# Prompt softmax in a hybrid attention decoder: the reciprocals' spread goes through memory, and the outputs are multiplied in SBUF

## The reference

```python
p, m, den = _softmax_stats(s, sink)        # p = exp(s - max), den = its sum (+ the sink's share)
o = jnp.einsum('nbcgqs,nbscd->nbqcgd', p.astype(vc.dtype), vc, preferred_element_type=jnp.float32)
o = o / jnp.transpose(den, (0, 1, 4, 2, 3))[..., None]
```

## Time and profile before

| what | us |
|---|---|
| median of three runs (lowest, highest) | 2282.36 (2281.73, 2285.25) |
| the profiled execution's own time | 2281.3 |
| its span in the profile | 2279.5 |
| TensorE busy | 2218.8 |
| VectorE busy | 961.8 |
| ScalarE busy | 658.9 |
| GpSimd busy | 137.5 |

### The profile page before, as it was taken

How to read it: one execution, slowest core, us unless ns; L and a number is a source line. 1 busy time by engine, 2 the same in 40 slices (tenths; PEclk the granted TensorE clock), 3 DMA queues, 4 the chain that set the end, 5 groups by cost and what they waited for, 6 DMA issues and landing times.

```text
span 2279.5 us, 33504 instructions
## 1 busy us (share of the span) xinstructions
PE 2218.8 (97%) x13723; PEld 1996.8 (88%) x13723; DVE 961.8 (42%) x1694; ACT 658.9 (29%) x1293; POOL 137.5 (6%) x216
## 2 busy tenths in 40 slices
PE   6999999898999999999999999989999999999998
PEld 6999877686789989899898998889989899898996
DVE  4120386575643424334243345663424334243346
ACT  4111496543432203122031223451303113031121
POOL 1000130000120000000000003330000000000001
PEclk9999999999999999999999999999999999999999
DMA  5230400398321202012020123230202102021023
GB/s 167 80 86 29 158 2 2 114 404 291 102 93 46 65 10 74 27 46 64 9 74 25 49 92 110 89 102 28 66 9 74 46 28 65 9 74 45 29 90 119
DMA packets 127934, 176.15 MB, mean 77 GB/s; under 512 B 14365, under 2 KB 96469, under 8 KB 127708
## 3 DMA queue, kind: packets, MB, share of 16 engines
q1 hardware_dynamic: 121644, 170.05, 22.7%
q10 hardware_dynamic: 6192, 4.72, 0.7%
HBM read 156.40 MB, written 18.58 MB: 77 GB/s over the span
## 4 chain that ended last, share of the span: by engine, by line
PE 76%; DMA 2%; DVE 1%; SPq 1%; issue 0%; ACT 0%; POOL 0%; DVEq 0%; POOLq 0%; ACTq 0%
PE ps L1731 33%; PE ps L1711 33%; PE ps L2606 4%; DMA sa_va<-cache_a_v 1%; PE ps L2555 1%; PE ps L2574 1%; PE ps L1390 1%; PE ps L1720 1%; PE ps L1447 1%; PE ps L1410 0%; DVE m_xT_lo L2361 0%; PE ps L2626 0%; DMA sa_kb<-cache_b_k 0%; SPq L654 0%; PE ps L1430 0%
## 5 line engine op out<-in xcount | busy, mean ns | idle before, releaser
L1675 DVE TENSOR_TENSOR t_y<-t_y,ps 128x512 f32<-128x512 f32 x288 | 197.7, 687 | 626.4 <-PE ps L1731 626.2
L1731 PE MATMUL ps<-t_w_hi,t_h_hi 128*128 128x512 f32 x1152 | 449.7, 390 | 2.9 <-DVE t_h_hi L1652 2.2
L1731 PE MATMUL ps<-t_w_lo,t_h_hi 128*128 128x512 f32 x1152 | 448.4, 389 | 0.0
L1731 PE MATMUL ps<-t_w_hi,t_h_lo 128*128 128x512 f32 x1024 | 398.4, 389 | 0.0
L1711 PE MATMUL ps<-m_xT_lo,t_w_hi 128*128 128x384 f32 x1488 | 327.9, 328 | 0.0
L1711 PE MATMUL ps<-m_xT_hi,t_w_lo 128*128 128x384 f32 x1488 | 327.9, 328 | 0.0
L1711 PE MATMUL ps<-m_xT_hi,t_w_hi 128*128 128x384 f32 x1488 | 327.8, 328 | 0.0
L1606 ACT ACTIVATE t_relu<-ps 128x384 f32<-128x384 f32 (+1 forms) x192 | 87.9, 458 | 809.4 <-PE ps L1731 776.7
L1636 DVE TENSOR_TENSOR t_w_lo<-t_raw,t_w_hi 128x1024 fp32r<-128x1024 f32 x128 | 155.4, 1224 | 276.5 <-ACT t_w_hi L1594 276.1
L1731 PEld LDWEIGHTS ps<-t_w_hi,t_h_hi 128*128 128x128 f32 x1152 | 216.2, 188 | 50.9 <-DVE t_h_hi L1652 3.1
L1711 PEld LDWEIGHTS ps<-m_xT_hi,t_w_hi 128*128 128x128 f32 x1488 | 254.7, 188 | 1.1
(11 more groups left out here) (224 smaller groups left out, 2476.0 us busy)
## 6 DMA issues: line engine op xcount, KB each, us to landing
t_raw<-mlp_w SPq DMA_DIRECT2D x128, 512.0 KB, 4.0
sa_kb<-cache_b_k SPq DMA_DIRECT2D x40, 512.0 KB, 8.9
sa_vb_even<-cache_b_v SPq DMA_DIRECT2D x20, 512.0 KB, 11.3
sa_vb_odd<-cache_b_v SPq DMA_DIRECT2D x20, 512.0 KB, 10.9
in_raw<-attn_w_in SPq DMA_DIRECT2D x6, 1024.0 KB, 5.6
t_rows<-scratch_x SPq DMA_DIRECT2D x12, 512.0 KB, 5.2
qT<-x_prompt SPq DMA_DIRECT2D x8, 512.0 KB, 3.6
t_rows<-x_prompt SPq DMA_DIRECT2D x8, 512.0 KB, 3.4
```

The source lines that it names most:

```text
L1675: self.nc.vector.tensor_tensor(part, part, self.core.ps[:, 6 + n % 2, :], ALU.add).then_inc(self.part_added, 1)
L1731: mm = self.nc.tensor.matmul(self.core.ps[:, 6 + half, :], a[:, k, t * P:t * P + P], w[:, k, half * 512:(half + 1) * 512], start=(k == 0 a ...
```

## The change

The spread groups leave the list of groups, and with them the four transposes, ScalarE's copy and the repeating copy. In a round, VectorE makes the reciprocals of 8 sums for 128 queries; SyncE waits for them, stores them turned (8 rows of 128, element by element) in a scratch tensor in memory, waits for the store's landing, and issues two loads which bring four rows each, repeated on 64 partitions, into `spread`. VectorE takes the outputs from PSUM by a plain copy into `qT`, and multiplies them there in place with `spread` in a new function, `normalise`, at the step u + 12 for a round that closes at unit u (or at the last step, 133). SyncE's new loop stands behind `load_early`. The number of other groups stays 112, their order stays, and their numbers, and so their places in the batches and PSUM banks, shift.

```diff
@@ -681,7 +681,7 @@
     leading_parts: object
 
 
-def prompt_attention(core, inp, qT, qT_offset, kaT, kbT, v, prompt_bias, sinks, load_sample, q_b, q_a):
+def prompt_attention(core, inp, qT, qT_offset, kaT, kbT, v, prompt_bias, sinks, load_sample, q_b, q_a, rden_rows):
 
 
 
@@ -710,8 +710,7 @@
     pT = core.at("pa_pT", base + Attend.PT, [P, 4, 4 * P])
     least = core.at("pa_least", base + Attend.LEAST, [P, PT, HEADS])
     den = core.at("pa_den", base + Attend.LEAST + 512, [P, PT, HEADS])
-    rden = core.at("pa_rden", base + Attend.LEAST + 1024, [P, NH * HD])
-    rden_one = core.at("pa_rden_one", base + Attend.SINK + 64, [P, 2 * PT, NH])
+    rden = core.at("pa_rden", base + Attend.SINK + 64, [P, 2 * PT, NH])
     spread = core.at("pa_spread", base + Attend.SPREAD, [P, 2, 4 * P])
     sink_in = core.sem("pa_sink_in")
     tables_in = [core.sem(f"pa_tables_in{x}") for x in range(3)]
@@ -722,8 +721,9 @@
     biased = core.sem("pa_biased")
     exped = core.sem("pa_exped")
     rden_made = core.sem("pa_rden_made")
-    rden_ready = core.sem("pa_rden_ready")
-    spread_ready = core.sem("pa_spread_ready")
+    rden_stored = core.sem("pa_rden_stored")
+    spread_in = [core.sem(f"pa_spread_in{x}") for x in range(2)]
+    normalised = core.sem("pa_normalised")
     turned = core.sem("pa_turned")
     copied = [core.sem("pa_copied_act"), core.sem("pa_copied_dve")]
     multiplied = core.sem("pa_multiplied")
@@ -761,18 +761,6 @@
     groups = []
     for u in range(0, U, 2):
         groups += [(u, g, min(2, n_tiles(u) - g)) for g in range(0, n_tiles(u), 2)]
-        if u + 1 in closing:
-            groups.append((u, 0, 0))
-
-    def is_spread(n):
-
-        return groups[n][2] == 0
-
-    spread_index = [n for n in range(len(groups)) if is_spread(n)]
-
-    def before(n):
-
-        return sum(not is_spread(m) for m in range(n))
 
     of_pair = {}
     for n, (u, _, _) in enumerate(groups):
@@ -828,20 +816,22 @@
         return u if wide(u) else u - 2
 
 
-    copier = [int(n % 2 == 1 and k > 0) for n, (u, _, k) in enumerate(groups)]
+    copier = [n % 2 for n in range(len(groups))]
     rounds = {u: x for x, u in enumerate(closing)}
 
-    def group_of(n):
-
-        return rounds[groups[n][0] + 1]
+    normalised_at = {}
+    for u in closing:
+        normalised_at.setdefault(min(u + 12, STEPS), []).append(u)
+
+    def outputs(u):
+
+        i, j, _ = parts_of(u)
+        group = j // 4
+        return qT[:, 4 * group:4 * group + 4, i * P:(i + 1) * P]
 
     def wait_for_copy(n):
 
-        if is_spread(n):
-            nc.tensor.wait_ge(spread_ready, group_of(n) + 1)
-        else:
-            mine = [copier[m] for m in range(n + 1) if not is_spread(m)]
-            nc.tensor.wait_ge(copied[copier[n]], mine.count(copier[n]))
+        nc.tensor.wait_ge(copied[copier[n]], copier[:n + 1].count(copier[n]))
 
 
     pieces = []
@@ -893,6 +883,16 @@
             sp.dma_start(bias_low[:, :, c], table_b[:, 0:5, c]).then_inc(tables_in[x], 16)
             sp.dma_start(bias_high[:, :, c], table_b[:, 5:NH, c]).then_inc(tables_in[x], 16)
         load_sample(sp)
+        for x in range(len(closing)):
+            sp.wait_ge(rden_made, x + 1)
+            sp.dma_start(rden_rows[x].rearrange("d q -> q d"), rden[:, x, :],
+                         allow_slow_non_contiguous=True).then_inc(rden_stored, 16)
+            sp.wait_ge(rden_stored, 16 * (x + 1))
+            if x >= 2:
+                sp.wait_ge(normalised, x - 1)
+            for half in range(2):
+                sp.dma_start(spread[half * HD:(half + 1) * HD, x % 2, :].rearrange("p (j c) -> p j c", j=4),
+                             rden_rows[x, half::2].partition_broadcast(HD)).then_inc(spread_in[x % 2], 16)
 
     def gpsimd(pool):
         for n in range(len(pieces)):
@@ -922,16 +922,9 @@
         def copy(n):
             u, _, k = groups[n]
             act.wait_ge(turned, n + 1)
-            if is_spread(n):
-                x = group_of(n)
-                if x >= 2:
-                    act.wait_ge(o_taken, x - 1)
-                nc.scalar.activation(spread[:, x % 2, :], core.ps[:, 4 + n % 2, :], ACT.Copy).then_inc(spread_ready, 1)
-                return
-            m = before(n)
-            if m >= 4:
-                act.wait_ge(multiplied, m - 3)
-            nc.scalar.activation(pT[:, m % 4, 0:2 * k * P], core.ps[:, 4 + n % 2, 0:2 * k * P],
+            if n >= 4:
+                act.wait_ge(multiplied, n - 3)
+            nc.scalar.activation(pT[:, n % 4, 0:2 * k * P], core.ps[:, 4 + n % 2, 0:2 * k * P],
                                  ACT.Copy).then_inc(copied[0], 1)
 
         act.wait_ge(inp.q_taken, inp.columns)
@@ -955,14 +948,18 @@
         def take_outputs(u):
 
             i, j, _ = parts_of(u)
-            group = j // 4
-            dve.wait_ge(multiplied, before(turned_after(u)))
+            dve.wait_ge(multiplied, turned_after(u))
+            dve.wait_ge(lo_done, lo_pieces(piece_no[i, j - 1] + 1))
+            nc.vector.tensor_copy(outputs(u), core.ps[:, 6 + j // 4, :].rearrange("p (j c) -> p j c", j=4)).then_inc(
+                o_taken, 1)
+
+        def normalise(u):
+
             x = rounds[u]
-            dve.wait_ge(spread_ready, x + 1)
-            dve.wait_ge(lo_done, lo_pieces(piece_no[i, j - 1] + 1))
-            nc.vector.tensor_tensor(qT[:, 4 * group:4 * group + 4, i * P:(i + 1) * P],
-                                    core.ps[:, 6 + group, :].rearrange("p (j c) -> p j c", j=4),
-                                    spread[:, x % 2, :].rearrange("p (j c) -> p j c", j=4), ALU.mult).then_inc(o_taken, 1)
+            dve.wait_ge(o_taken, x + 1)
+            dve.wait_ge(spread_in[x % 2], 32 * (x // 2 + 1))
+            nc.vector.tensor_tensor(outputs(u), outputs(u), spread[:, x % 2, :].rearrange("p (j c) -> p j c", j=4),
+                                    ALU.mult).then_inc(normalised, 1)
 
         dve.wait_ge(sink_in, 16)
         nc.vector.tensor_scalar(neg_sink[:], sink_b[:], -1.0, None, ALU.mult).then_inc(sink_ready, 1)
@@ -990,27 +987,21 @@
             for n in (n for batch in batches_at(step) for n in batch):
                 if copier[n] == 1:
                     dve.wait_ge(turned, n + 1)
-                    m = before(n)
-                    if m >= 4:
-                        dve.wait_ge(multiplied, m - 3)
+                    if n >= 4:
+                        dve.wait_ge(multiplied, n - 3)
                     k = groups[n][2]
-                    nc.vector.tensor_copy(pT[:, m % 4, 0:2 * k * P],
+                    nc.vector.tensor_copy(pT[:, n % 4, 0:2 * k * P],
                                           core.ps[:, 4 + n % 2, 0:2 * k * P]).then_inc(copied[1], 1)
             if step - 2 in closing:
                 x = rounds[step - 2]
                 i, j, _ = parts_of(step - 2)
                 d = 2 * j + 2 - NH
                 dve.wait_ge(exped, step - 1)
-                one = rden_one[:, x, :]
-                nc.vector.reciprocal(one, den[:, i, d:d + NH]).then_inc(rden_made, 1)
-                if x >= 1:
-                    dve.wait_ge(turned, spread_index[x - 1] + 1)
-                dve.wait_ge(rden_made, x + 1)
-                nc.vector.tensor_copy(rden[:].rearrange("p (h d) -> p h d", h=NH),
-                                      one.rearrange("p (h o) -> p h o", o=1).to_broadcast([P, NH, HD])
-                                      ).then_inc(rden_ready, 1)
+                nc.vector.reciprocal(rden[:, x, :], den[:, i, d:d + NH]).then_inc(rden_made, 1)
             for u in taken_at.get(step, ()):
                 take_outputs(u)
+            for u in normalised_at.get(step, ()):
+                normalise(u)
 
     def tensor(pe):
         def scores(u):
@@ -1043,13 +1034,6 @@
             u, g, k = groups[n]
             if n >= 2:
                 wait_for_copy(n - 2)
-            if is_spread(n):
-                pe.wait_ge(rden_ready, group_of(n) + 1)
-                for p in range(4):
-                    last = nc.tensor.transpose(core.ps[:, 4 + n % 2, p * P:(p + 1) * P], rden[:, p * P:(p + 1) * P],
-                                               core.identity[:])
-                last.then_inc(turned, 1)
-                return
             if g == 0:
                 pe.wait_ge(exped, u + 2)
             for half in range(2):
@@ -1076,7 +1058,7 @@
                     c = (half * k + t) * P
                     last = nc.tensor.matmul(core.ps[half * HD:(half + 1) * HD, 6 + j // 4,
                                                     j % 4 * P:(j % 4 + 1) * P],
-                                            v[:, kt, vc:vc + HD], pT[:, before(n) % 4, c:c + P],
+                                            v[:, kt, vc:vc + HD], pT[:, n % 4, c:c + P],
                                             start=(g + t == 0), stop=(g + t == n_tiles(u) - 1))
             last.then_inc(multiplied, 1)
 
@@ -2715,7 +2697,7 @@
```

(6 more changed lines are left out.)

## The result

The changed kernel takes 2373.22 us, the median of four runs (2369.52 to 2379.66), against 2282.05 us before (2280.85 to 2285.25, four runs). The ratio is 1.0397 with a 95% interval of 1.0382 to 1.0412: 91 us slower, where 2284.0 was forecast and 2297 was the range's top. The profiled execution of after took 2379.66 us, with a span of 2377.8.

What follows compares the result with a forecast made beforehand. TensorE, busy 97% of the span, was taken as the bound. -5.0 - 6.5 + 0.8 + 10.3 + 2.0 = +1.6 us on 2281.3 gave 2282.9, 2284.0 for the median; own range 2278 to 2287, wider 2273 to 2297.

Steps and rivals of the forecast that it cites:

- the price of the store: Each round's reciprocal store on SyncE, 1024 elements of 4 bytes: 2.5 us to landing, low end 1.6, high end 5.0.
- Small packets cost little: DMA claim behind the store's price: some 16.5 ns a packet and engine, from a window mostly of packets up to 256 bytes.
- Rival (a): Prompt attention: 4-byte writes make the chain too long, several rounds stall; 2290 us at 8.2, near 2305 at 10.4; chance 0.19.
- the tight 7.0 us: Shortest ten steps from reciprocal to normalising multiply, claimed to cover the 5.7 us chain of store and loads.
- Rival (d): The change acts otherwise, for instance loads reading each row 64 times are slow at the source; within (a)'s chance of 0.19.
- a chain of some 5 us: Store and loads together, estimated by the skill page's fixed cost of about 2.0 us per DMA.
- The first stall: First round's normalising multiply near 273 us: VectorE waits 12.1 us behind early loads; booked 10.3, ends 8.1 and 14.2.
- The clock: After the first round's idle, TensorE's granted clock falls to 0.50; booked 2.0 us, low end 0.
- The savings: Prompt attention's dropped transposes, batches and waits: 5.0 us before 336 us, 6.5 us after.
- breaks: TensorE's two gaps in each batch; eight fewer batches at 0.33 us save 2.6 us at most.
- The wait for the outputs' taking: TensorE's 2.9 us wait at L1077 for outputs to be taken, claimed to go with the spread groups.
- the tail: Stage's end: a second pass over the last outputs before the barrier, +0.7 us, with its semaphore +0.8.

Runs made afterwards that it cites:

- the first experiment: The changed kernel with each round's reciprocals stored as 128 rows of 32 bytes instead of 1024 elements of 4 bytes; 2287.66 us, ratio 1.0011 to before.

## Why the prediction was wrong, point by point

**The step that failed is the price of the store**, "Small packets cost little". It took the rate at which packets pass the DMA engines in the earlier trace rows, 16.5 ns, and priced the store as 1.6 us + 56 packets. The packets' rate was no worse than that: the digits of after's strip, 0.9 of a slice of 0.425 us for 64 packets an engine, make some 6 ns a packet, an estimate from rounded digits, and once the elements are spaced the store lands in 2.8 us. What the row couldn't show is the landing of writes that lie side by side: 11.7 us, as if each of the 56 further packets took 0.18 us. The high end of the term, 5.0 us, was set by doubling twice a price of the wrong kind; the rows that it stood on had loads of 256-byte packets into SBUF and a store of rows of 512 bytes, never a narrow write into memory. The sentence "the trace has no store of 4-byte elements into memory, so the high end is open" was the true one, and the range closed it at 60 ns.

**Rival (a) was the right one, with the wrong size.** Its mechanism is what the trace shows: several multiplies wait, everything behind them on VectorE too. It was priced at 8.2 and 10.4 us of chain; measured is about 16: in the round of 381.13 us the loads go out at 393.05 and the multiply starts at 397.47 us. That is over the tight 7.0 us and over the 9 us of the last round, so eleven rounds stall, not three or four. Five don't, four of them in the stage's last third, where 19 to 26 us lie between the store's issue and the multiply. The store is not the whole chain: the loads, booked at 3.1 us, took up to 12.2 us in after. Rival (d), loads that are slow by their pattern, is out: with rows of 32 bytes the same loads land in 2.9 us.

Of the store's layout the Trainium skill ("DMA: Bandwidth & Descriptors", "Rules for kernel authors") says to make the last dimension contiguous; the first experiment agrees, 11.7 us become 1.9. The page's fixed cost of about 2.0 us per DMA, which it fits to DMAs issued by GpSimd and by which the prediction named a chain of some 5 us, is near the 1.9 us of the rows of 32 bytes and 0.8 below the 2.8 us of the spaced elements. It misses the 11.7 us of the adjacent ones, and there the measurement decides.

**The first stall**: forecast 12.1 us; 13.0 with rows of 32 bytes and 20.1 in after, where the crowded store took 19.2 us instead of 13.8, some 5 of the 7 us of difference. Moving the early loads cut it to 2.9. The step holds, and so does its price: stall and clock were booked at 10.3 + 2.0 us, and moving the loads won 12. (The stall's low end, 8.1, comes to 8.4 by its own terms, 12.1 - 0.9 - 2.8; nothing hangs on it.)

**The clock**: forecast 0.50 behind the first stall. After, from 276 us in tens (columns as the earlier trace rows):

```profile
276.00:286.00 10.00, 0.00 (x0) 0.00 (x0) 0.00 (x0) 0.00 (x0) 0.00 (x0) 0.56 0.53 188
286.00:296.00 10.00, 2.44 (x14) 1.71 (x14) 3.68 (x20) 2.74 (x11) 0.73 (x1) 0.50 0.22 27
296.00:306.00 10.00, 9.20 (x83) 7.41 (x82) 4.32 (x20) 5.83 (x22) 3.19 (x4) 0.75 0.04 3
306.00:316.00 10.00, 0.89 (x6) 0.71 (x6) 2.32 (x13) 1.25 (x5) 0.00 (x0) 0.59 0.16 26
```

It falls to 0.50, the 1.2 GHz level, while TensorE is idle, has a mean of 0.75 in the ten microseconds in which TensorE is busy again, and is at 0.59 with the second stall. The price was right for one stall and grows with eleven: against the stage without long stalls (157.11 us busy at 0.98) TensorE's 177.90 us at 0.82 are 20.8 us more for the same work. Its idle time is 92.9 for 13.6 us, and 20.8 + 79.3 is the 100.1 us between the two stages.

**The savings**: forecast 11.5 us less 0.8, 2272 for the median without the first stall. Measured with rows of 32 bytes and later loads: 9.8 us below before (2285.34 - 2275.58; by the ratio's interval 6 to 13). The total holds, and so does its cover: with a store of 1.9 us only the first multiply waits. The terms behind the total don't. TensorE's busy time in the stage fell from 168.21 to 157.11 us, by 11.1, where 64 transposes were priced at 6.9 us, by their weight loads. The matmuls themselves were busy for longer (before, 240 to 440 us):

```profile
L1049 PE MATMUL ps<-identity,pa_rden 128*128 128x128 f32 x64 | 10.5, 289 | 1.8 <-ACT pa_pT L934 1.7
```

TensorE's idle time, from which up to 2.6 us of breaks and 4.6 us of waits were to go, went from 11.1 to 13.6 us, with the 2.9 us stall in it. The wait for the outputs' taking did go, as forecast, but the breaks don't show. That the total came out near all the same is in part luck.

**The deferred multiply**: booked +0.8 for the tail and nothing else; the multiply alone, without the repeating copy's going, cost 3 us, by its interval 0.7 to 5.3. The 0.8 is at its lower edge; perhaps a part of VectorE's work in the crowded first half isn't hidden.

**What went unnamed**: the end of the stage. The prediction said that the last reciprocal is 9 us ahead of its use; with a chain of 16 us TensorE idles from 517 us to the barrier, and the next stage starts below full clock. After and before, the first 10 us behind the barrier:

```profile
527.00:537.00 10.00, 8.85 (x57) 7.86 (x61) 5.34 (x17) 4.00 (x13) 0.75 (x4) 0.69 0.70 216
```

```profile
435.00:445.00 10.00, 7.88 (x77) 5.97 (x77) 5.93 (x18) 4.00 (x13) 0.75 (x4) 1.00 0.66 214
```

In the hundred microseconds behind the barrier the granted clock is 0.94 against 1.00. Most of the 6.1 us that after loses behind the stage would be this; it wasn't taken apart further.

## What to carry to other kernels

Don't price a transposing store by its packets: ask what the narrowest contiguous piece in memory is, and if it is 4 bytes, turn the data on an engine first, or give it rows of 32 bytes, the narrowest that was quick here. Where a resource has no row in the trace, the open end of its term is the place where the range must stay open; a multiple of another row's price isn't a bound. A round trip through memory on the path needs the cover of its whole chain in every round, and its place in the queue behind bulk loads is worth as much as its own length.

## What the runs showed of the hardware that was not expected

- 1024 writes of 4 bytes into memory, side by side, land 11.7 us after issue; 8 bytes apart 4.5, 16 apart 3.4, 64 apart 2.8; 512 of them side by side 8.7 (medians). The records of the packets end within 1.3 us all the same, so the profile shows the cost only as time in which nothing moves.
- Such a store delays independent loads issued behind it on the same queue: 13.3 to 18.7 us from issue to use instead of 4.2 to landing.
- After has a few waits in the stage whose releaser is given as "remote". The longest, 4.5 us on VectorE, ends at 520.35, 1.5 us before a crowded store's landing. Neither before nor the kernel with rows of 32 bytes has such a wait in the stage. The profile lists instruction queues among its DMA queues (page of after: q8 instruction, 69 packets); that the loading of instructions is held up as well would fit, and no run tested it.
- Open: by what piece of memory the writes get in each other's way, and how. The spacings fall off smoothly, and a query's eight elements written from one partition are slow too, which speaks against a conflict between partitions' writes as the whole cause.
